# FFN up projection with the activation stationary and the weight streamed, the product turned by VectorE

## The reference

```python
def rmsnorm(x, g):
    y = x * lax.rsqrt(jnp.mean(x * x, axis=-1, keepdims=True) + EPS)
    return y * g

def swiglu_ffn(h, w_gate_up, w_down):
    gate, up = jnp.split(h @ w_gate_up, 2, axis=-1)
    return (jax.nn.silu(gate) * up) @ w_down

# D_MODEL = 2048, D_FF = 5632, SEQ = 256
for i in range(2):
    h = h + mixer_i(rmsnorm(h, mixer_norm))
    h = h + swiglu_ffn(rmsnorm(h, ffn_norm[i]), ffn_w_gate_up[i], ffn_w_down[i])
return rmsnorm(h, final_norm)
```

## Time and profile before

| | |
|---|---|
| median of three runs | 2159.73 us (2159.62 to 2161.22) |
| the profiled execution | 2160.21 us |
| its span | 2158.5 us |
| TensorE busy | 2144.3 us, 99% |
| VectorE busy | 1211.9 us, 56% |
| ScalarE busy | 1062.1 us, 49% |
| read from HBM | 399.55 MB, 186 GB/s |

### The profile page before, as it was taken

The page is one execution under the profiler, slowest core; times in us unless marked ns, Lnnn a source line. Parts: engine busy times, 40 slices in busy tenths (PEclk is TensorE's granted clock), DMA queues, the critical chain, the costliest instruction groups (busy, mean ns, idle before and its releaser), DMA issues.

```text
span 2158.5 us, 30354 instructions
## 1 busy us (share of the span) xinstructions
PE 2144.3 (99%) x10993; PEld 1824.8 (85%) x10993; DVE 1211.9 (56%) x1216; ACT 1062.1 (49%) x1212; POOL 15.9 (1%) x29
## 2 busy tenths in 40 slices
PE   9999999999999999999999999999999999999998
PEld 7888888888888888888888888888888888888886
DVE  5556565555655556544445565555655656554444
ACT  5555555554545545444445444454545555544443
POOL 1000000000000000000000000000000000000000
PEclk9999999999999999999999999999999999999999
DMA  7555545566566565655556665556565666655554
GB/s 259 181 168 164 178 152 174 177 194 186 172 197 185 183 188 173 202 188 195 191 189 205 186 197 176 186 180 197 177 201 178 200 188 187 192 193 193 191 193 146
DMA packets 207128, 402.43 MB, mean 186 GB/s; under 512 B 12305, under 2 KB 12897, under 8 KB 206689
## 3 DMA queue, kind: packets, MB, share of 16 engines
q1 hardware_dynamic: 206352, 398.51, 58.2%
q0 software_dynamic: 688, 3.18, 0.4%
q10 hardware_dynamic: 32, 0.01, 0.0%
HBM read 399.55 MB, written 2.10 MB: 186 GB/s over the span
## 4 chain that ended last, share of the span: by engine, by line
PE 99%; DVE 0%; issue 0%; ACT 0%; POOLq 0%; POOL 0%; DVEq 0%; ACTq 0%
PE acc L1022 17%; PE acc L1024 17%; PE acc L1023 17%; PE tp L1191 15%; PE acc L1191 15%; PE tp L1193 8%; PE acc L1193 8%; PE tp L1032 1%; PE tp L1281 0%; PE tp L1088 0%; PE tp L1078 0%; PE tp L1101 0%; PE tp L1079 0%; PE tp L1080 0%; PE tp L1102 0%
## 5 line engine op out<-in xcount | busy, mean ns | idle before, releaser
L636 DVE TENSOR_TENSOR w_lo<-raw,w_hi 128x1024 fp32r<-128x1024 f32 x751 | 910.2, 1223 | 702.2 <-ACT w_hi L343 701.5
L343 ACT ACTIVATE w_hi<-raw 128x1024 fp32r<-128x1024 f32 x751 | 790.3, 1060 | 797.9 <-PE acc L1024 426.8
L1191 PE MATMUL acc<-xT,w_hi 128*128 128x512 f32 x1408 | 524.6, 395 | 0.0
L1191 PE MATMUL tp<-xT,w_hi 128*128 128x512 f32 x1408 | 524.3, 395 | 0.0
L1193 PE MATMUL tp<-xT,w_lo 128*128 128x256 f32 x1408 | 394.8, 280 | 0.0
L1193 PE MATMUL acc<-xT,w_lo 128*128 128x256 f32 x1408 | 394.8, 280 | 0.0
L1022 PE MATMUL acc<-w_hi,hid_hi 128*128 128x512 f32 x944 | 368.5, 390 | 0.9 <-DVE hid_lo L711 0.9
L1024 PE MATMUL acc<-w_hi,hid_lo 128*128 128x512 f32 x944 | 367.5, 389 | 0.0
L1023 PE MATMUL acc<-w_lo,hid_hi 128*128 128x512 f32 x944 | 367.3, 389 | 0.0
L1191 PEld LDWEIGHTS tp<-xT,w_hi 128*128 128x128 f32 x1408 | 263.9, 187 | 61.9
L1191 PEld LDWEIGHTS acc<-xT,w_hi 128*128 128x128 f32 x1408 | 264.0, 187 | 61.7
(11 more groups left out here) (144 smaller groups left out, 855.7 us busy)
## 6 DMA issues: line engine op xcount, KB each, us to landing
raw<-in_ffn_w_gate_up SPq DMA_DIRECT2D x352, 512.0 KB, 4.3
raw<-in_ffn_w_down SPq DMA_DIRECT2D x176, 512.0 KB, 3.8
raw<-in_sb_w_qkv SPq DMA_DIRECT2D x95, 512.0 KB, 4.3
raw<-in_gm_w_in SPq DMA_DIRECT2D x64, 512.0 KB, 4.4
raw<-in_sb_w_o SPq DMA_DIRECT2D x32, 512.0 KB, 4.0
raw<-in_gm_w_o SPq DMA_DIRECT2D x32, 512.0 KB, 4.1
h<-in_x SPq DMA_DIRECT2D x3, 512.0 KB, 9.4
gain_bc<-in_gm_v_norm POOLq DMA_DIRECT2D x1, 1024.0 KB, 7.9
```

Source lines behind the costliest of these rows:

```text
L343: nc.scalar.activation(w_hi[:, p % RING], raw[:, p % RING], ACT.Copy).then_inc(hi_ready, 1)
L636: nc.vector.tensor_tensor(w_lo[:, p % RING], raw[:, p % RING], w_hi[:, p % RING].bitcast(f32), ALU.subtract).then_inc(lo_ready, 1)
L1191: nc.tensor.matmul(dst, w_hi[:, p % RING, k, ns], xT[:, kt].rearrange("p v t -> p (v t)"), start=(kt == 0), stop=False)
```

## The change

The turned form goes. ffn_up uses `piece` as the other projections do, with gate in one half of acc and up in the other (chunk 0 and 1). ScalarE reads gate from acc with Silu and the per-partition scale rstd in one step (two activations of 128 x 512), and VectorE multiplies up by rstd and gate in one step (two scalar_tensor_tensor of 128 x 512) into res. The product has the sequence in the partitions and has to be transposed for the down projection. VectorE does that with 16 transposes a round, each of 32 partitions and eight blocks of 32 x 32, from res into tp[1] in PSUM; two of them stand behind the split in each of pieces 0 to 7 of the next round. ScalarE reads hid_hi from tp[1] at piece 8, VectorE writes hid_lo at piece 9. rstd_row, spread, the four matmuls of L1213, the copies of the low part, the additions and the products by rstd_row go. The numbers that res_ready counts to are lower by one in the down projections, since the last round no longer counts there, and the final down projection's loop of two on TensorE is written out. The transposes behind piece 1 stay. The last round of a layer is turned in pieces 0 to 7 of the down projection.

```diff
+    Q = 32
...
@@ -74,12 +75,8 @@
         raw = sb("raw", [P, RING, KP, CH])
         w_hi = sb("w_hi", [P, RING, KP, CH], f32r)
         w_lo = sb("w_lo", [P, RING, KP, CH], f32r)
-        gate = sb("gate", [P, TC, S])
+        gate = sb("gate", [P, RT, CH])
         res = sb("res", [P, RT, CH])
-        hidden = res[:, :, :].rearrange("p r (k t) -> p (r k) t", t=S)
-
-        spread = gate[:, 0].rearrange("p (r t) -> p r t", r=RT)
...
-
-        GATE_BANKS = (acc[:, 0:RT * CH], tp[1][:, :])
-        UP_BANKS = (acc[:, RT * CH:2 * RT * CH], tp[0][:, :])
-
-        def parts(bank_pair, which):
-
-            return bank_pair.rearrange("p (k v t) -> p k v t", k=2, v=2)[:, :, which]
...
 
-            def rstd_row_out(layer):
-                act.wait_ge(row_out[layer], 1)
-                nc.scalar.activation(rstd_row[:, :], UP_BANKS[0][:, 0:S], ACT.Copy).then_inc(row_ready[layer], 1)
-
-            def low_out(layer, dst, banks, t_end, done):
-
-                act.wait_ge(used, AT_UP[layer] + t_end)
-                for n in range(2):
-                    last = nc.scalar.activation(dst[:, 2 * n:2 * n + 2, :], parts(banks[n], 1), ACT.Copy)
-                last.then_inc(done[layer], 1)
-
             def gate_silu(layer, i):
-                act.wait_ge(gate_scaled[layer], i + 1)
-                nc.scalar.activation(gate[:, :, :], gate[:, :, :], ACT.Silu).then_inc(gate_ready[layer], 1)
+                act.wait_ge(used, AT_UP[layer] + PD + i * (2 * PD))
+                for r in range(RT):
+                    last = nc.scalar.activation(gate[:, r], acc_at(0, r), ACT.Silu,
+                                                scale=rstd[:, 1 + 2 * layer, r:r + 1])
+                last.then_inc(gate_ready[layer], 1)
 
             def hidden_high(layer, i):
-                act.wait_ge(f_res[layer], i + 1)
-                nc.scalar.activation(hid_hi[:, bass.ds(i * TC, TC), :], hidden, ACT.Copy).then_inc(f_hi[layer], 1)
+                act.wait_ge(f_turned[layer], i + 1)
+                nc.scalar.activation(hid_hi[:, bass.ds(i * TC, TC), :],
+                                     tp[1][:, :].rearrange("p (k t) -> p k t", k=TC), ACT.Copy).then_inc(f_hi[layer], 1)
...
-                    if p == PD - 2:
-                        rstd_row_out(layer)
-                    if p == PD - 1:
-                        low_out(layer, gate, GATE_BANKS, PD, gate_low)
-                with act.Fori(0, NF - 1) as i:
+                    if t == PD - 1:
+                        act.wait_ge(n_rstd[m], 1)
+                        gate_silu(layer, 0)
+                with act.Fori(1, NF) as i:
                     for t in range(2 * PD):
-                        ahead(AT_UP[layer] + PD, i, 2 * PD, t)
-                        if t == 0:
+                        ahead(AT_UP[layer], i, 2 * PD, t)
+                        if t == PD - 1:
+                            act.wait_ge(f_res[layer], i)
                             gate_silu(layer, i)
-                        if t == PD - 1:
-                            low_out(layer, hidden, UP_BANKS, i * (2 * PD) + 2 * PD, up_low)
-                        if t == PD + 1:
-                            hidden_high(layer, i)
-                        if t == 2 * PD - 1:
-                            low_out(layer, gate, GATE_BANKS, i * (2 * PD) + 3 * PD, gate_low)
-                            act.wait_ge(f_lo[layer], i + 1)
-                for p in range(PD):
-                    ahead(AT_UP[layer] + (2 * NF - 1) * PD, 0, PD, p)
-                    if p == 0:
-                        gate_silu(layer, NF - 1)
-                low_out(layer, hidden, UP_BANKS, 2 * NF * PD, up_low)
+                        if t == PD:
+                            hidden_high(layer, i - 1)
 
             ffn_up(0)
             for it in range(ND // 2):
                 for t in range(2 * PF):
                     ahead(AT_DOWN[0], it, 2 * PF, t)
-                    if t == 1 and it == 0:
+                    if t == PD and it == 0:
                         hidden_high(0, NF - 1)
                     if t == 1 and it > 0:
                         norm_chunk(2, 2 * it - 1)
...
 
-            def rstd_spread(layer):
-                m = 1 + 2 * layer
-                dve.wait_ge(n_rstd[m], 1)
+            def up_out(layer, i):
+                dve.wait_ge(used, AT_UP[layer] + 2 * PD + i * (2 * PD))
+                dve.wait_ge(gate_ready[layer], i + 1)
                 for r in range(RT):
-                    last = nc.vector.tensor_scalar(spread[:, r], ident[:, :], 0.0, rstd[:, m, r:r + 1], ALU.mult,
-                                                   ALU.add)
-                last.then_inc(spread_ready[layer], 1)
-
-            def add_high(dst, banks, done):
-
-                for n in range(2):
-                    part = dst[:, 2 * n:2 * n + 2, :]
-                    last = nc.vector.tensor_tensor(part, parts(banks[n], 0), part, ALU.add)
-                last.then_inc(done, 1)
-
-            def by_rstd(t, done):
-                nc.vector.tensor_tensor(t, t, rstd_row[:, :].unsqueeze(1).to_broadcast([P, TC, S]),
-                                        ALU.mult).then_inc(done, 1)
-
-            def gate_out(layer, i):
-                dve.wait_ge(gate_low[layer], i + 1)
-                add_high(gate, GATE_BANKS, gate_summed[layer])
-                dve.wait_ge(gate_summed[layer], i + 1)
-                by_rstd(gate[:, :, :], gate_scaled[layer])
-
-            def up_out(layer, i, read, seen):
-                dve.wait_ge(up_low[layer], i + 1)
-                add_high(hidden, UP_BANKS, read)
-                dve.wait_ge(read, seen)
-                by_rstd(hidden, up_scaled[layer])
-                dve.wait_ge(gate_ready[layer], i + 1)
-                dve.wait_ge(up_scaled[layer], i + 1)
-                nc.vector.tensor_tensor(hidden, hidden, gate[:, :, :], ALU.mult).then_inc(f_res[layer], 1)
+                    last = nc.vector.scalar_tensor_tensor(
+                        out=res[:, r], in0=acc_at(1, r), scalar=rstd[:, 1 + 2 * layer, r:r + 1], in1=gate[:, r],
+                        op0=ALU.mult, op1=ALU.mult)
+                last.then_inc(f_res[layer], 1)
+
+            def turn_hidden(layer, i, n):
+                if n == 0:
+                    dve.wait_ge(f_res[layer], i + 1)
+                for b in (2 * (n % 2), 2 * (n % 2) + 1):
+                    a = n // 2
+                    last = nc.vector.transpose(
+                        tp[1][b * Q:(b + 1) * Q, :].rearrange("p (k r q t) -> p k r q t", k=TC, r=RT, q=4)[:, :, :, a],
+                        res[a * Q:(a + 1) * Q, :, :].rearrange("p r (k q c) -> p k r q c", k=TC, q=4)[:, :, :, b])
+                if n == 7:
+                    last.then_inc(f_turned[layer], 1)
 
             def hidden_low(layer, i):
                 dve.wait_ge(f_hi[layer], i + 1)
                 ks = bass.ds(i * TC, TC)
-                nc.vector.tensor_tensor(hid_lo[:, ks, :], hidden, hid_hi[:, ks, :].bitcast(f32),
-                                        ALU.subtract).then_inc(f_lo[layer], 1)
+                nc.vector.tensor_tensor(hid_lo[:, ks, :], tp[1][:, :].rearrange("p (k t) -> p k t", k=TC),
+                                        hid_hi[:, ks, :].bitcast(f32), ALU.subtract).then_inc(f_lo[layer], 1)
 
             def ffn_up(layer):
                 m = 1 + 2 * layer
-                for p in range(PD):
-                    ahead(AT_UP[layer], 0, PD, p)
-                    if p == 1:
+                for t in range(2 * PD):
+                    ahead(AT_UP[layer], 0, 2 * PD, t)
+                    if t == 1:
                         gained_low(m, ND - 1, ND)
-                    if p == 2:
+                    if t == 2:
                         mean_square(m, ND)
-                    if p == 3:
-                        rstd_spread(layer)
-                    if p == PD - 1:
-                        dve.wait_ge(row_ready[layer], 1)
-                        gate_out(layer, 0)
-                with dve.Fori(0, NF - 1) as i:
+                    if t == 2 * PD - 1:
+                        dve.wait_ge(n_rstd[m], 1)
+                        up_out(layer, 0)
+                with dve.Fori(1, NF) as i:
                     for t in range(2 * PD):
-                        ahead(AT_UP[layer] + PD, i, 2 * PD, t)
-                        if t == PD - 1:
-                            up_out(layer, i, up_summed[layer], i + 1)
+                        ahead(AT_UP[layer], i, 2 * PD, t)
+                        if t < PD:
+                            turn_hidden(layer, i - 1, t)
                         if t == PD + 1:
-                            hidden_low(layer, i)
+                            hidden_low(layer, i - 1)
                         if t == 2 * PD - 1:
-                            gate_out(layer, i + 1)
-                for p in range(PD):
-                    ahead(AT_UP[layer] + (2 * NF - 1) * PD, 0, PD, p)
```

(84 more changed lines are left out.)

22 lines of the change are left out of this document (6 added, 16 removed).

## The result

The changed kernel takes 2130.98 us (median of four, 2130.61 to 2131.05) against 2160.43 of the kernel before in the same comparison: ratio 0.9864, 95% interval 0.9849 to 0.9878. The forecast was 2131.5. The profiled execution took 2131.03 us with a span of 2129.3, which is 29.2 us shorter than the span before.

What follows compares the result with a forecast made beforehand. TensorE was taken as the bound, busy 2144.3 of 2158.5 us. Shorter up projections save 18.9 + 9.8 = 28.7 us, all other terms nothing: 2160.2 - 28.7 = 2131.5 us, range 2127 to 2143.

Steps and rivals of the forecast that it cites:

- The plain form in the up projections: TensorE: 176 pieces of 12 matmuls at 0.2267 us, plus one interruption, make each up projection 479.7 us.
- 18.9 and 9.8 us saved: TensorE's up projections shorten from 498.60 (layer 0) and 489.53 us (layer 1) to 479.7, together 28.7 us.
- The transposes by TensorE behind piece 1, 0.90 us: The eight transposes that stay in each up projection interrupt the plain form for 0.90 us.
- VectorE's transposes: Pieces 0 to 7: 0.48 us each taken, between 0.288 and 0.96; both ends cost nothing in time.
- 5.8 us of slack: Time a split can be late before TensorE waits for its w_lo: 8.16 - 2.35 us.
- The third rival: VectorE can't keep up in pieces 0 to 7; at 1.28 us a transpose, 60 us lost, 2191 us; chance 0.09.
- ScalarE: A round swaps four copies and a Silu for two activations; table loads stay; piece 11's split 2.65 us late, costing nothing.
- The new waits: TensorE waits for gate_ready at t = 0 and f_res at t = 8; both covered by eight pieces, costing nothing.
- the last round: Its f_lo moves from t = 1 to t = 9 of the down projection, wanted at t = 20; costs nothing.
- a slower rhythm of the plain form (A): Up projections step by 0.2315 us: 10.1 us a layer, 2141.6 us for one, 2151.8 for both; chance 0.07.
- Only columns (B): A piece costs its 6144 columns whatever the matmul count; only L1213 and its restart go, 0.9 us: 2159.3; chance 0.04.
- VectorE too slow (C): Same as the third rival: TensorE stalls for w_lo in each round's first half; 2191 us, chance 0.09.

Runs made afterwards that it cites:

- halved: The changed kernel with each 512-column matmul of the up projections cut into two of 256, with a weight load each: 2186.91 us.
- f32r control: The changed kernel with all matmuls of an up-projection piece on one stationary xT tile and one w_hi tile, in f32r: 2130.82 us.

## Why the prediction was right, step by step

*The plain form in the up projections:* forecast 479.7 us each, measured 479.65 in both. The step of 0.2267 us, read in a down projection, holds in another stage, beside other work in PSUM. The halved and the f32r control runs show that it is a price of columns and of matmuls.

*18.9 and 9.8 us saved:* measured 18.95 and 9.88. The run without L1213 splits them: 9.5 us in layer 0 (498.60 to 489.08) are the slow rhythm and L1213 itself, 0.45 us in layer 1 are L1213, and 9.4 us in each layer, from 489.08 to 479.65, are the fewer matmuls. The slow rhythm's share needed no cause: the prediction took it from the trace as it stood. Its own account (from L1213 on) leaves out that both layers also began in that rhythm.

*The transposes by TensorE behind piece 1, 0.90 us:* 0.91 from the 22 sets of the run that turns the product on TensorE. The prediction named this only for the set that stays. That the change would have been worth 9 us without VectorE's turning wasn't said there; it is the larger part of why it paid.

*VectorE's transposes:* 0.48 taken, 0.456 measured, both in the cover. The upper bound of 0.96 would have been covered too, by the same reasoning; the run with six a piece shows where the cover ends: at 3.6 us of VectorE a piece the lag outgrows the 5.8 us of slack within eight pieces. The third rival was the right mechanism with a price it didn't have, and it had the place wrong: TensorE's stops come in the second half of a round, not in the first.

*ScalarE:* this step was wrong, without effect on the time. It said that the table loads stay. They did not: the earlier trace rows shows 20 at L507, and the groups of before have 23 more at L343, 1.28 us each; the changed kernel has two for its Silu and three for its splits in all. So the split of piece 11 was late by the two activations alone (1.2 us, from 686.21 to 687.37) and not by 2.65.

*The new waits, the last round, the DMAs, the written-out loop:* nothing each. TensorE has no idle time in the up projections: 2112 steps of 0.2267 and one interruption of 0.90 make 479.7.

*The rivals:* a slower rhythm of the plain form (A) was in no run; all seven kernels with the plain form in f32r and 512 columns ran at 0.2267 wherever nothing stopped them. Only columns (B) fell with the halved run. VectorE too slow (C) came about only with three times as many transposes: with six a piece the kernel was 10 us slower than the one before.

## What to carry to other kernels

Where TensorE is the bound, compare two forms of a product by the time from one start to the next in a stage of the same trace, and count matmuls as well as columns: here the same 6144 columns cost 2.72, 2.77 or 2.83 us in 12 or 16 matmuls. A layout that needs a transpose is worth it if an engine that waits can do it, and the slack of that engine can be worked out from when its result is ready and when it is wanted. An alternation of long and short matmuls can settle in a slower rhythm after an interruption, so read each stage before a difference is put down to an edit.

## What the runs showed of the hardware that was not expected

- The same alternation of 512 and 256 columns runs in two steady rhythms, 0.347 and 0.353 us a pair, at the same granted clock, and stays in it for the rest of the stage, 170 pieces. An interruption can change it. In six of six places the rhythm behind the small matmuls depended on the pattern of pairs ahead of them (347, 347, 346 ns: slow; 350, 343: fast), and not on the interruption's length, 0.45 or 0.9 us.
- A matmul of f32r operands costs 13.3 ns beside its columns at 256 and at 512; one of bf16 2 to 3 ns at 512 (0.216 us).
- A set of eight 128x128 transposes costs TensorE 0.79 us and 0.11 of restart.
- VectorE's 32x256 transposes from SBUF to PSUM start 0.46 to 0.48 us after one that went to another group of 32 partitions, and 0.33 to 0.37 after one that went to the same.
- ScalarE's table loads for the splits and the Silu fell from 43 to 5 though the same two functions alternate. The changed kernel calls Silu once before each loop; whether that is the cause wasn't tried.
